# A two-block transformer kernel: order of splits, key scaling and copies in the delta rule, and one wait before out1

## The chip, the cores and the metric

One NeuronCore of a Trainium2 chip runs the whole program, all in fp32. The metric is device microseconds of one execution. The median of three runs of the kernel before is 2344.24 us (2344.18 to 2345.7). Engines: PE is TensorE, DVE VectorE, ACT ScalarE, POOL GpSimd, SP SyncE.

## The reference, cut to what matters

Input x has 512 tokens of 1024 features. A first block has two layers (Fourier and neighbourhood attention, then a gated convolution; each followed by cross attention over 256 memory rows and a convolutional feed-forward). A second block has retention, a gated delta rule and a feed-forward. The two parts that the change touches:

```python
def short_gated_conv_mixer(h, w_in, conv_w, w_out):      # layer 1: in1, then out1
    z = h @ w_in
    gate_b, gate_c, u = z[..., :D], z[..., D:2*D], z[..., 2*D:]
    return (gate_b * dwconv3_centred(gate_c * u, conv_w)) @ w_out

# second block, delta rule: 8 heads of 128, chunks of 128 tokens
qkv = silu(causal_dwconv(concat([dq, dk_, dv_]), dn_conv_w))   # 4 taps per channel
cq, ck = l2norm(cq), l2norm(ck)
g = -exp(dn_a_log) * softplus(da + dn_dt_bias); beta = sigmoid(db)
G = cumsum(g) in a chunk; L = where(causal, exp(G_i - G_j), 0)
A = where(strict, (beta k_i . k_j) * L, 0); attn = (q_i . k_j) * L
T = inverse(I + A)                                  # lower triangular, 128 x 128
u, w = T @ (beta v), T @ (beta k exp(G))
for each chunk: v_new = u - w S; o = q_dec S + attn v_new; S = S d + k_dec^T v_new
```

## The kernel before, in words

**Weights.** Every product with a weight matrix is three fp32r products: w_hi x_hi, w_hi x_lo, w_lo x_hi. Weights come in units of 256 x 512 (512 KB) through a ring of 5 slots (`RING`). For each unit SyncE waits until TensorE has used the slot's last unit and issues the load, ScalarE copies it to `w_hi` (`split`, L624), GpSimd subtracts it for `w_lo` (`lo`, L555), and TensorE does 24 matmuls of 128x512 (`products`, L1067, one line for all: L1081). The units have one order, and each engine does its share in it. ScalarE has the splits between its other work by hand: `split_to(n)` (L630) splits all units before n, and `LEAD` is 4, so `split_to(u + LEAD)` splits up to four units ahead of what TensorE has finished when it has finished u units.

**Engines and semaphores.** Each engine has one queue in program order. All order between engines is by `wait_ge` on counting semaphores; an engine that waits holds all that stands behind it. SyncE's queue holds the weight loads and the DMAs of `diagonal_blocks` and `inverses` (L461, L469), which are placed behind the load of a given unit (L519 to L523).

**The delta stage.** First unit `dab` (projections for beta and decay) and `decay_rows`: ScalarE and VectorE compute rows of 8 x 512, ScalarE stores two of them to `rows_dram`, TensorE transposes four (`decay_columns`, behind the third unit of the first group), ScalarE copies them to TC. `spread(i)` loads the rows of two heads, repeated on all 128 partitions, to GB (1 MB). Then `delta(0)` and `delta(1)`, called half 0 and half 1 here, four heads each. A half has 16 units from `u0 = first["dkqv{q}"]`: keys (u0 to u0+3) into four PSUM banks A, queries (u0+4 to +7) into banks B, then values (+8 to +11) and the `gated` projection (+12 to +15) into B. For keys, queries, values in turn VectorE scales the banks by the norm R into GX (`evacuate`, L2043) and does 16 convolution taps of 128x512 (`taps`, L2049: four multiplies at L2056, twelve multiply-adds at L2059). For keys and queries ScalarE then has silu (L933) and square (L937), TensorE sums the squares into banks A (`squares`, L1427), ScalarE has logarithm and exponential (`inverse_norm`, L939) and VectorE multiplies (`normalise`, L2080). `ages`, `decays` and `with_beta` make the decays DL and AT of two heads at a time. TensorE has `keys_by_keys` (L1438) behind the third unit of the values, `keys_transposed` behind the first unit of `gated` and `keys_by_queries` (L1457) behind its third. VectorE multiplies `keys_by_keys` into AT (L2140); SyncE writes AT to DRAM and reads the 16x16 diagonal blocks back to FSA; VectorE inverts them (`block_inverses`, L2086); SyncE brings them as PKM and PKT (`inverses`), GpSimd spreads them to MM and MT (`expand`, L602), and TensorE and VectorE go by levels to the inverse of 128. ScalarE copies the transposed keys with a factor to KD (`scaled_rows`, L947, line L951), which frees the banks for `keys_by_queries`. At last the scan over four chunks.

**Before out1.** The last two groups of `in1` write banks 0 to 3 and 4 to 7. VectorE scales banks 4 to 7 into TY (L1918), multiplies (L1920), ScalarE copies to YH (L822), VectorE subtracts to YL (L1922). TensorE waits for TY's scaling (L1358) and then starts `out1`, first half into banks 0 to 3, second into 4 to 7.

Of the kernel before, what the change touches and what calls it, by code (L numbers as in the profile page):

```python
# [24 lines left out]
P = 128  # L25
D = 1024
KT = D // P
T = 512
# [65 lines left out]
def program(nc, ins, out):  # L94
    ctx = ExitStack()
    with ctx:
# [67 lines left out]
        def pcol(name, i=0, n=1):  # L164
            c = PARAM_COLS[name][0] + i
            return par[:, c:c + n]
# [281 lines left out]
        def _(sp):  # L448
# [34 lines left out]
            for name, mat, nk, groups in phases:  # L483
# [25 lines left out]
                for g in range(len(groups)):  # L509
# [4 lines left out]
                    for k in range(per):  # L514
# [4 lines left out]
                        for q in range(2):  # L519
                            if u == first[f"gated{q}"] + 3:  # L520
                                diagonal_blocks(q)
                            elif u == first[f"gated{q}"] + 4:
                                inverses(q)  # L523
# [27 lines left out]
        def _(pool):  # L551
# [50 lines left out]
            def expand(q):  # L602
                for i, (pk, m) in enumerate(((PKM, MM), (PKT, MT))):
                    pool.wait_ge(pk_loaded, 16 * (2 * q + i + 1))
                    for hh in range(4):
                        nc.gpsimd.tensor_tensor(
                            m[:, hh, :].rearrange("p (n b c) -> p n b c", n=NCH, c=FIRST),
                            pk[:, 4 * hh:4 * hh + 4, :].unsqueeze(2).broadcast_to([P, NCH, P // FIRST, FIRST]),
                            BD[:, :, :].unsqueeze(1).broadcast_to([P, NCH, P // FIRST, FIRST]), ALU.mult).then_inc(mx_pool, 1)
# [11 lines left out]
        def _(act):  # L621
# [266 lines left out]

            def decay_rows():
# [10 lines left out]
                nc.scalar.activation(sm[0:DN_H, 80:81], pcol("a_log")[0:DN_H, :], ACT.Exp).then_inc(ab_act, 1)  # L900
                act.wait_ge(ab_dve, 9)
# [4 lines left out]
                nc.scalar.dma_start(rows_dram[1], BR[:, :]).then_inc(rows_saved, 16)  # L906
                act.wait_ge(ab_t, 1)
                nc.scalar.activation(TC[:, :, :, :], ps[:, 1, 0:4 * NCH * DN_H].rearrange("p (a n h) -> p a n h", a=4, n=NCH),
                                     ACT.Copy).then_inc(ab_act, 1)

            def spread(i):

                act.wait_ge(rows_saved, 32)
                src = bass.AP(rows_dram.tensor, 2 * i * T, [[0, P], [DN_H * T, 2], [T, 2], [1, T]])
                nc.scalar.dma_start(GB[:, :, :, :], src).then_inc(gb_loaded, 16)

            def delta(q):
# [37 lines left out]
                if q == 0:  # L955
                    decays(0)
                else:
                    split_to(u0 + 2 + LEAD)
                    decays(0)
                    split_to(u0 + 3 + LEAD)  # L960
                    out_norm(0)
# [3 lines left out]
                spread(2 * q + 1)  # L965
                silu(0, KN)
                if q:
                    act.wait_ge(do_n, q)
                square(0, KN, SQk)
                decays(1)  # L970
# [8 lines left out]
                split_to(u0 + 14 + LEAD)  # L979
# [37 lines left out]
            def block2():  # L1017
# [21 lines left out]
                spread(0)  # L1039
# [26 lines left out]
        def _(pe):  # L1066
# [174 lines left out]
            def residual(name, units, xh, xl, ready, after=None):  # L1241
                u = first[name]
                group(u, units, 0, xh, xl, ready, after=after)
                if after is not None:
                    pe.wait_ge(m_ln, 1)
# [96 lines left out]
            for l in range(2):  # L1342
                if l == 0:
                    pe.wait_ge(na_pt, 2 * NA_H)
                    residual("out0", 4, YH, YL, lambda kt: [(f2_lo, kt + 1) if kt < NA_H else (na_lo, kt - NA_H + 1)],
                             after=mem_stat)
                else:
# [10 lines left out]
                    pe.wait_ge(cm_dve, 18 + 16)  # L1358
                    residual("out1", 4, YH, YL, lambda kt: [(cm_dve, 18 * (kt // 4) + 18)])
# [282 lines left out]
        def _(dve):  # L1642
# [391 lines left out]
            def delta(q):  # L2034
# [8 lines left out]
                def evacuate(i):  # L2043
# [3 lines left out]
                    nc.vector.tensor_tensor(GX, banks(inputs[i][2]), over(R[:, :], 4), ALU.mult).then_inc(dq_dve, 1)  # L2047

                def taps(i, start, stop):  # L2049
                    g, dst, _ = inputs[i]  # L2050
                    for n in range(start, stop):
                        back, c = n // 4, n % 4
                        tap = pcol("dn_conv", (3 - back) * 3 * DN_H + g * DN_H + 4 * q + c)
                        if back == 0:
                            dve.wait_ge(dq_dve, nd + 17 * i + 1)
                            nc.vector.tensor_tensor(dst[:, c, :], GX[:, c, :], tap.broadcast_to([P, T]), ALU.mult).then_inc(dq_dve, 1)  # L2056
                        else:
                            dve.wait_ge(dq_dve, nd + 17 * i + n - 2)
                            nc.vector.scalar_tensor_tensor(out=dst[:, c, back:T], in0=GX[:, c, 0:T - back], scalar=tap,  # L2059
# [74 lines left out]
                taps(1, 0, 12)  # L2134
                normalise(0, KN, LNk, 1.0)
                taps(1, 12, 16)
# [293 lines left out]
```

## Time and profile before

| what | value |
|---|---|
| runs | 2344.24 us median (2344.18, 2344.24, 2345.7) |
| profiled execution | 2348.35 us, its span 2346.5 us |
| mean granted TensorE clock | 0.988 of full speed |
| PE, PEld busy | 2280.2 us (97%), 1877.5 us (80%) |
| DVE, ACT, POOL busy | 965.2 (41%), 859.8 (37%), 990.0 (42%) |
| DMA | 222.96 MB, mean 95 GB/s |
| delta stage | about 1487 to 1885 us from the span's start |

The span is from the first to the last recorded instruction of the profiled execution; its own time is 1.85 us longer. An engine is busy while one of its instructions runs. What an engine waited for is put down to the instruction whose semaphore came last. The chain of waits is followed back from the last instruction. Times of rows are microseconds from the span's start.

### The profile page before, as it was taken

Reading aid. Unit: us, or ns where it says so; the run is one execution under the profiler, and the core shown is the slowest. Engines: PE = TensorE matmul, PEld = TensorE weight load, DVE = VectorE, ACT = ScalarE, POOL = GpSimd, SP = SyncE. Lnnn points to the kernel's source line nnn. Section 1 sums busy time; section 2 is a strip of 40 time slices with the busy share of each in tenths; the row PEclk is TensorE's granted clock in tenths of the full one; section 3 lists DMA queues with packets and bytes.
Section 4 is the critical chain, followed back from the end, with each engine's and each line's share of the span. In section 5 each row is a group of like instructions: output and inputs, shape, how many; then the busy total and the mean of one; then the engine's idle time right before and its main releaser. Section 6 shows DMA issues by size and latency. Waiting matters only on the chain.

```text
span 2346.5 us, 24834 instructions
## 1 busy us (share of the span) xinstructions
PE 2280.2 (97%) x10550; PEld 1877.5 (80%) x10550; DVE 965.2 (41%) x1165; ACT 859.8 (37%) x1042; POOL 990.0 (42%) x416
## 2 busy tenths in 40 slices
PE   9999999999999999999999999888998999999997
PEld 7888788888887887888887858777877888888886
DVE  4241324441144213434226441387487332766601
ACT  4354333332322434433345273343352434322221
POOL 5437234544444642444444404244133243464542
PEclk9999999999999999999999999999999999999999
DMA  6325123323332431333333303432131133333332
GB/s 225 95 64 170 54 81 99 98 92 98 99 96 91 154 100 49 95 99 98 92 111 121 95 16 93 112 89 67 56 108 46 53 102 124 99 96 94 98 99 72
DMA packets 159997, 222.96 MB, mean 95 GB/s; under 512 B 24064, under 2 KB 85632, under 8 KB 159632
## 3 DMA queue, kind: packets, MB, share of 16 engines
q1 hardware_dynamic: 158336, 216.63, 30.1%
q10 hardware_dynamic: 1552, 4.76, 0.6%
q8 instruction: 83, 1.36, 0.2%
q14 instruction: 26, 0.21, 0.0%
HBM read 214.50 MB, written 6.85 MB: 94 GB/s over the span
## 4 chain that ended last, share of the span: by engine, by line
PE 89%; DVE 6%; DMA 2%; ACT 2%; issue 1%; POOL 0%; SPq 0%; ACTq 0%; DVEq 0%
PE ps L1081 75%; PE ps L1275 2%; PE ps L1278 2%; PE ps L1291 1%; PE ps L1314 1%; DVE QN L2056 1%; DVE QN L2059 1%; PE ps L1385 1%; PE ps L1463 1%; PE ps L1398 1%; PE ps L1457 1%; PE ps L1438 0%; PE ps L1589 0%; DMA w_raw<-w_in 0%; DVE FSU L2096 0%
## 5 line engine op out<-in xcount | busy, mean ns | idle before, releaser
L559 POOL TENSOR_TENSOR w_lo<-w_raw,w_hi 128x1024 fp32r<-128x1024 f32 x378 | 959.1, 2547 | 1313.4 <-ACT w_hi L628 1313.1
L628 ACT ACTIVATE w_hi<-w_raw 128x1024 fp32r<-128x1024 f32 x378 | 394.9, 1056 | 896.0 <-DMA w_raw<-w_in 140.7
L1081 PE MATMUL ps<-XH,w_hi 128*128 128x512 f32 x1784 | 701.7, 393 | 15.2 <-POOL w_lo L559 13.2
L1081 PE MATMUL ps<-XH,w_lo 128*128 128x512 f32 x1784 | 696.2, 390 | 0.0
L1081 PE MATMUL ps<-XL,w_hi 128*128 128x512 f32 x1784 | 695.8, 390 | 0.0
L1081 PE MATMUL ps<-HID,w_hi 128*128 128x512 f32 x1728 | 534.5, 391 | 2.5 <-DVE TY L1918 2.4
L1081 PEld LDWEIGHTS ps<-XH,w_hi 128*128 128x128 f32 x1784 | 336.0, 188 | 89.7 <-issue 17.6
L1081 PEld LDWEIGHTS ps<-XL,w_hi 128*128 128x128 f32 x1784 | 336.0, 188 | 71.3 <-issue 2.4
L1081 PEld LDWEIGHTS ps<-XH,w_lo 128*128 128x128 f32 x1784 | 335.7, 188 | 70.1
L1081 PEld LDWEIGHTS ps<-HID,w_hi 128*128 128x128 f32 x1728 | 325.0, 188 | 71.3 <-DVE TY L1918 2.8
L1081 PE MATMUL ps<-HID,w_lo 128*128 128x512 f32 x864 | 336.9, 390 | 0.0
L1679 DVE TENSOR_TENSOR H<-ps,H 128x512 f32<-128x512 f32 x64 | 42.4, 683 | 362.7 <-PE ps L1081 311.7
L1081 PEld LDWEIGHTS ps<-HID,w_lo 128*128 128x128 f32 x864 | 162.5, 188 | 34.0
L1855 DVE TENSOR_TENSOR GP<-ps,R 128x1024 f32<-128x1024 f32 x16 | 19.6, 1224 | 179.0 <-PE ps L1081 179.0
L1806 DVE TENSOR_TENSOR QX<-ps,R 128x2048 f32<-128x2048 f32 x4 | 9.2, 2291 | 157.3 <-PE ps L1081 157.3
L2235 DVE SCALAR_TENSOR_TENSOR CV<-GP,par,CV 128x512 f32<-128x512 f32 x88 | 72.0, 888 | 0.0
L2227 DVE TENSOR_TENSOR GP<-ps,R 128x2048 f32<-128x2048 f32 x11 | 25.2, 2292 | 76.6 <-PE ps L1081 76.6
L638 ACT ACTIVATE SQ<-H 128x512 f32<-128x512 f32 x56 | 35.3, 631 | 55.3 <-DVE ACC L1651 30.3
L810 ACT ACTIVATE EG<-CV,par 128x512 f32<-128x512 f32 x32 | 22.2, 725 | 85.7 <-DVE CV L1864 85.7
L1651 DVE TENSOR_TENSOR ACC<-ACC,SQ 128x512 f32<-128x512 f32 x62 | 45.0, 726 | 3.2 <-ACT SQ L638 0.9
L1864 DVE SCALAR_TENSOR_TENSOR CV<-GP,par,CV 128x512 f32<-128x512 f32 x64 | 43.7, 740 | 0.0
L1873 DVE TENSOR_TENSOR HID<-HF,HID 128x1024 fp32r<-128x1024 f32 x16 | 35.5, 2219 | 18.0 <-ACT HID L814 18.0
(356 smaller groups left out, 2259.8 us busy)
## 6 DMA issues: line engine op xcount, KB each, us to landing
w_raw<-w_in SPq DMA_DIRECT2D x72, 512.0 KB, 3.8
w_raw<-ffn_w_up SPq DMA_DIRECT2D x128, 256.0 KB, 2.9
w_raw<-w_up SPq DMA_DIRECT2D x88, 256.0 KB, 3.1
w_raw<-xa_wkv SPq DMA_DIRECT2D x32, 512.0 KB, 3.7
w_raw<-ffn_w_down SPq DMA_DIRECT2D x32, 512.0 KB, 3.8
w_raw<-w_in_c SPq DMA_DIRECT2D x24, 512.0 KB, 3.8
w_raw<-w_down SPq DMA_DIRECT2D x22, 512.0 KB, 3.8
w_raw<-xa_wq SPq DMA_DIRECT2D x16, 512.0 KB, 3.8
```

The source lines that it names most:

```text
L559: nc.gpsimd.tensor_tensor(w_lo[:, s, :, :], w_raw[:, s, :, :], w_hi[:, s, :, :].bitcast(F32), ALU.subtract).then_inc(lo_done, 1)
L628: nc.scalar.activation(w_hi[:, s, :, :], w_raw[:, s, :, :], ACT.Copy).then_inc(hi_done, 1)
L638: nc.scalar.activation(ACC[:, :] if c == 0 else SQ[:, :], H[:, c, :], ACT.Square).then_inc(sq_done, 1)
L1081: mm = nc.tensor.matmul(ps[:, bank + m, :], a, b, start=start and j == 0 and n == 0, stop=stop and j == 1 and n == 2)
L1275: mm = nc.tensor.matmul(ps[:, bank + m, 0:NMEM], wt[:, m * P:(m + 1) * P], xt, start=begin, stop=end)
L1278: mm = nc.tensor.matmul(ps[:, bank + m, :], xt[:, m * P:(m + 1) * P], wt, start=begin, stop=end)
L1651: nc.vector.tensor_tensor(ACC[:, :], ACC[:, :], SQ[:, :], ALU.add).then_inc(acc_done, 1)
L1679: nc.vector.tensor_tensor(H[:, c, :], ps[:, (c + flip) % 8, :], H[:, c, :], ALU.add).then_inc(h_upd, 1)
L1864: nc.vector.scalar_tensor_tensor(out=CV[:, q, :], in0=GP[:, q, i:T + i], scalar=tap(i, q), in1=CV[:, q, :], op0=ALU.mult, op1=ALU.add).the ...
L1873: nc.vector.tensor_tensor(HID[:, 2 * g + nf:2 * g + nf + 2, :], HF[:, :, :], HID[:, 2 * g:2 * g + 2, :].bitcast(F32), ALU.subtract).then_i ...
L2227: nc.vector.tensor_tensor(GP4[:, :, 2:T + 2], banks(bank), over(R[:, :], 4), ALU.mult).then_inc(up2_dve, 1)
L2235: nc.vector.scalar_tensor_tensor(out=CV4[:, q, :], in0=GP4[:, q, i:T + i], scalar=of(w0 + 2 * nf * i, q), in1=CV4[:, q, :], op0=ALU.mult, ...
```

## The change

ScalarE gets splits at new places: two between the decay rows, and single ones ahead of `decays(0)` of half 0, of the keys' silu and of `decays(1)`; one split fewer stands ahead of the KD copies. `spread(0)` moves ahead of the `TC` copy. The keys are scaled in place in PSUM (`banks(A)`) and tapped from there; queries and values go by GX as before. `normalise` of the keys follows 6 taps of the queries and not 12. On SyncE `inverses` moves behind the load of the next unit, and GpSimd waits for PKM and PKT together. `out1` waits for TY's scaling ahead of its second half; ahead of its first it waits for the bank's own reader.

```diff
--- before.py
+++ after.py
@@ -519,7 +519,7 @@
                         for q in range(2):
                             if u == first[f"gated{q}"] + 3:
                                 diagonal_blocks(q)
-                            elif u == first[f"gated{q}"] + 4:
+                            elif u == first[f"gated{q}"] + 5:
                                 inverses(q)
                         if name == "out0" and (g, k) == (0, per - 1):
 
@@ -601,7 +601,7 @@
             pool.wait_ge(vc_done, 8)
             def expand(q):
                 for i, (pk, m) in enumerate(((PKM, MM), (PKT, MT))):
-                    pool.wait_ge(pk_loaded, 16 * (2 * q + i + 1))
+                    pool.wait_ge(pk_loaded, 32 * (q + 1))
                     for hh in range(4):
                         nc.gpsimd.tensor_tensor(
                             m[:, hh, :].rearrange("p (n b c) -> p n b c", n=NCH, c=FIRST),
@@ -886,6 +886,12 @@
                         act.wait_ge(ret_ro, h)
                     nc.scalar.activation(RN[:, :], RLN[:, :], ACT.Exp, scale=-0.5).then_inc(ret_rn, 1)
 
+            def spread(i):
+
+                act.wait_ge(rows_saved, 32)
+                src = bass.AP(rows_dram.tensor, 2 * i * T, [[0, P], [DN_H * T, 2], [T, 2], [1, T]])
+                nc.scalar.dma_start(GB[:, :, :, :], src).then_inc(gb_loaded, 16)
+
             def decay_rows():
 
                 B1, A1, A3, SPR, BEG, EGL, EG8 = [rows[i][:, :] for i in (0, 1, 2, 3, 4, 5, 6)]
@@ -898,21 +904,18 @@
                 act.wait_ge(ab_act, 3)
                 nc.scalar.activation(A3, A3, ACT.Ln, bias=1.0).then_inc(ab_act, 1)
                 nc.scalar.activation(sm[0:DN_H, 80:81], pcol("a_log")[0:DN_H, :], ACT.Exp).then_inc(ab_act, 1)
+                split_to(first["dab"] + 2 + LEAD)
                 act.wait_ge(ab_dve, 9)
                 nc.scalar.activation(EG8, GR[:, :], ACT.Exp).then_inc(ab_act, 1)
                 act.wait_ge(ab_dve, 14)
                 nc.scalar.activation(EGL, EGL, ACT.Exp).then_inc(ab_act, 1)
                 nc.scalar.dma_start(rows_dram[0], GR[:, :]).then_inc(rows_saved, 16)
                 nc.scalar.dma_start(rows_dram[1], BR[:, :]).then_inc(rows_saved, 16)
+                spread(0)
+                split_to(first["dab"] + 3 + LEAD)
                 act.wait_ge(ab_t, 1)
                 nc.scalar.activation(TC[:, :, :, :], ps[:, 1, 0:4 * NCH * DN_H].rearrange("p (a n h) -> p a n h", a=4, n=NCH),
                                      ACT.Copy).then_inc(ab_act, 1)
-
-            def spread(i):
-
-                act.wait_ge(rows_saved, 32)
-                src = bass.AP(rows_dram.tensor, 2 * i * T, [[0, P], [DN_H * T, 2], [T, 2], [1, T]])
-                nc.scalar.dma_start(GB[:, :, :, :], src).then_inc(gb_loaded, 16)
 
             def delta(q):
                 u0 = first[f"dkqv{q}"]
@@ -953,6 +956,7 @@
                         last.then_inc(rows_act, 1)
 
                 if q == 0:
+                    split_to(u0 + 3 + LEAD)
                     decays(0)
                 else:
                     split_to(u0 + 2 + LEAD)
@@ -963,10 +967,12 @@
                 act.wait_ge(dp_eg, 4 * q + 2)
                 act.wait_ge(dp_be, 4 * q + 2)
                 spread(2 * q + 1)
+                split_to(u0 + 6 + LEAD)
                 silu(0, KN)
                 if q:
                     act.wait_ge(do_n, q)
                 square(0, KN, SQk)
+                split_to(u0 + 7 + LEAD)
                 decays(1)
                 split_to(u0 + 8 + LEAD)
                 inverse_norm(0, LNk)
@@ -976,7 +982,7 @@
                 square(1, QN, SQq)
                 split_to(u0 + 12 + LEAD)
                 inverse_norm(1, LNq)
-                split_to(u0 + 14 + LEAD)
+                split_to(u0 + 13 + LEAD)
                 act.wait_ge(dp_be, 4 * q + 4)
                 act.wait_ge(dp_eg, 4 * q + 4)
                 scaled_rows(KD, 3, 16 * q + 4)
@@ -1036,7 +1042,6 @@
                                          ACT.Sigmoid).then_inc(gr_act, 1)
                 split_to(first["dab"] + 1 + LEAD)
                 decay_rows()
-                spread(0)
                 delta(0)
                 delta(1)
                 for g in range(2):
@@ -1238,11 +1243,11 @@
                     fourier(s + 2)
             values(2 * NA_H - 1)
 
-            def residual(name, units, xh, xl, ready, after=None):
+            def residual(name, units, xh, xl, ready, after=None, second=None):
                 u = first[name]
                 group(u, units, 0, xh, xl, ready, after=after)
-                if after is not None:
-                    pe.wait_ge(m_ln, 1)
+                if second is not None:
+                    pe.wait_ge(*second)
                 group(u + units, units, 4, xh, xl)
 
             def mem_stat():
@@ -1343,7 +1348,7 @@
                 if l == 0:
                     pe.wait_ge(na_pt, 2 * NA_H)
                     residual("out0", 4, YH, YL, lambda kt: [(f2_lo, kt + 1) if kt < NA_H else (na_lo, kt - NA_H + 1)],
-                             after=mem_stat)
+                             after=mem_stat, second=(m_ln, 1))
                 else:
                     u0 = first["in1"]
                     for g in range(6):
@@ -1355,8 +1360,9 @@
 
                                 pe.wait_ge(cm_dve, 18 * ((g - 2) // 3) + (1, 2, 16)[(g - 2) % 3])
                             group(u0 + 4 * g, 4, 4 * (g % 2), XH, XL)
-                    pe.wait_ge(cm_dve, 18 + 16)
-                    residual("out1", 4, YH, YL, lambda kt: [(cm_dve, 18 * (kt // 4) + 18)])
+                    pe.wait_ge(cm_dve, 18 + 2)
+                    residual("out1", 4, YH, YL, lambda kt: [(cm_dve, 18 * (kt // 4) + 18)],
+                             second=(cm_dve, 18 + 16))
                 kv(l)
 
                 pe.wait_ge(kv_out, 4 * l + 3)
@@ -2044,19 +2050,21 @@
                     dve.wait_ge(w_used, u0 + 4 * i + 4)
                     if nd + i:
                         dve.wait_ge(dq_dve, nd + 17 * i)
-                    nc.vector.tensor_tensor(GX, banks(inputs[i][2]), over(R[:, :], 4), ALU.mult).then_inc(dq_dve, 1)
+                    x = banks(A) if i == 0 else GX
+                    nc.vector.tensor_tensor(x, banks(inputs[i][2]), over(R[:, :], 4), ALU.mult).then_inc(dq_dve, 1)
 
                 def taps(i, start, stop):
                     g, dst, _ = inputs[i]
+                    x = banks(A) if i == 0 else GX
                     for n in range(start, stop):
                         back, c = n // 4, n % 4
                         tap = pcol("dn_conv", (3 - back) * 3 * DN_H + g * DN_H + 4 * q + c)
                         if back == 0:
                             dve.wait_ge(dq_dve, nd + 17 * i + 1)
-                            nc.vector.tensor_tensor(dst[:, c, :], GX[:, c, :], tap.broadcast_to([P, T]), ALU.mult).then_inc(dq_dve, 1)
+                            nc.vector.tensor_tensor(dst[:, c, :], x[:, c, :], tap.broadcast_to([P, T]), ALU.mult).then_inc(dq_dve, 1)
                         else:
                             dve.wait_ge(dq_dve, nd + 17 * i + n - 2)
-                            nc.vector.scalar_tensor_tensor(out=dst[:, c, back:T], in0=GX[:, c, 0:T - back], scalar=tap,
+                            nc.vector.scalar_tensor_tensor(out=dst[:, c, back:T], in0=x[:, c, 0:T - back], scalar=tap,
                                                            in1=dst[:, c, back:T], op0=ALU.mult, op1=ALU.add).then_inc(dq_dve, 1)
 
                 def ages(pr):
@@ -2131,9 +2139,9 @@
                 ages(1)
                 evacuate(1)
                 with_beta(1)
-                taps(1, 0, 12)
+                taps(1, 0, 6)
                 normalise(0, KN, LNk, 1.0)
-                taps(1, 12, 16)
+                taps(1, 6, 16)
                 for hh in range(4):
                     dve.wait_ge(kv_pe, 16 * q + hh + 1)
                     dve.wait_ge(dp_be, 4 * q + hh + 1)
```

## Rows read from the trace of the kernel before

**Rows 1.** The page, part 1: busy us (share of the span) and instructions.

```profile
PE 2280.2 (97%) x10550; PEld 1877.5 (80%) x10550; DVE 965.2 (41%) x1165; ACT 859.8 (37%) x1042; POOL 990.0 (42%) x416
```

**Rows 2.** TensorE's waits, whole span: us in total, times, longest.

```profile
PE ps L1081 <- DVE TY L1918: 2.4, 1, 2.4
```

**Rows 3.** The same waits, stretch 1480 to 1670 (half 0).

```profile
PE ps L1081 <- POOL w_lo L559: 10.1, 2, 8.3
PE ps L1457 <- ACT KD L951: 5.8, 1, 5.8
PE ps L1438 <- DVE KN L2083: 4.9, 1, 4.9
```

**Rows 4.** The same waits, stretch 1670 to 1860 (half 1).

```profile
PE ps L1457 <- ACT KD L951: 7.3, 1, 7.3
PE ps L1081 <- POOL w_lo L559: 3.1, 1, 3.1
PE ps L1438 <- DVE KN L2083: 1.9, 1, 1.9
```

**Rows 5.** A stretch: length, busy PE, PEld, DVE, ACT, POOL, PEclk, DMA share, GB/s.

```profile
1775.00:1789.00 14.00, 7.07 (x36) 6.97 (x37) 6.24 (x10) 10.26 (x21) 11.26 (x8) 0.63 0.25 92
```

**Rows 6.** The chain of waits in the delta stage: start, us, what.

```profile
1492.35 16.32 PE ps L1081 x72
...
1509.80 6.93 DMA GB<-rows_dram
...
1523.68 24.04 PE ps L1081 x96
...
1574.50 6.01 PE ps L1438 x32
...
1581.25 5.04 DMA at_dram<-AT
...
1602.53 5.44 DMA w_raw<-w_in
...
1613.32 5.39 PE ps L1457 x32
...
1626.58 3.84 PE ps L1463 x32
...
1742.14 5.45 PE ps L1438 x32
...
1781.93 6.37 PE ps L1457 x32
```

**Rows 7.** ScalarE in order of time: start, us, line, tiles [idle before].

```profile
1500.41 0.20 ACT L900 ACTIVATE sm<-par 8x1 f32<-8x1 f32 x1
...
1520.06 3.88 ACT L628 ACTIVATE w_hi<-w_raw 128x1024 fp32r<-128x1024 f32 x4
...
1608.96 4.22 ACT L951 ACTIVATE KD<-ps,TC 128x128 f32<-128x128 f32 x16
```

**Rows 8.** GpSimd in order of time.

```profile
1550.02 16.88 POOL L559 TENSOR_TENSOR w_lo<-w_raw,w_hi 128x1024 fp32r<-128x1024 f32 x6 [18.12 <-ACT w_hi L628]
...
1618.48 5.06 POOL L606 TENSOR_TENSOR MT<-PKT,BD 128x512 f32<-128x512 f32 x4
```

**Rows 9.** VectorE in order of time.

```profile
1553.33 11.32 DVE L2056 TENSOR_TENSOR QN<-H,par 128x512 f32<-128x512 f32 x4
...
1603.80 2.35 DVE L2083 SCALAR_TENSOR_TENSOR QN<-QN,LNq 128x1024 f32<-128x1024 f32 x2
...
1702.63 8.00 DVE L2059 SCALAR_TENSOR_TENSOR KN<-H,par,KN 128x511 f32<-128x511 f32 x12
```

**Rows 10.** Two VectorE lines reading PSUM: ns min/median/max, first and last start.

```profile
L1679 DVE TENSOR_TENSOR H<-ps,H x64: 673/682/692, 157.4 to 2332.5; 128x512 f32<-128x512 f32 x64
...
L1985 DVE SCALAR_TENSOR_TENSOR RO<-ps,par,RN x8: 739/742/751, 1362.8 to 1401.5; 128x512 f32<-128x512 f32 x8
```

**Rows 11.** VectorE in order of time, before out1.

```profile
740.57 2.29 DVE L1922 TENSOR_TENSOR HID<-TY,HID 128x2048 fp32r<-128x2048 f32 x1 [1.98 <-ACT HID L822]
```

## The prediction

> **What bounds the kernel now.** Read first the busy row of the page: TensorE is busy 97% of the span [rows 1], so a change can save only what TensorE idles, or what it runs slowly. Next the waits of TensorE, over the span and then in each half of the delta stage: one wait of 2.4 us before `out1` [rows 2]; in half 0, 10.1 us for `w_lo` in two waits (8.3 the longest, so 1.8 the other), 5.8 us for KD and 4.9 us for the normalised keys [rows 3]; in half 1, 3.1, 7.3 and 1.9 us [rows 4]. Together 35.5 us. The third view is the table of stretches: around the 7.3 us wait the mean granted clock is 0.63 [rows 5], that is, most of the stretch lies at 1.2 GHz and not at 2.4, behind an idle TensorE. So a wait costs more than its length. The chain of waits prices that [rows 6]. 72 matmuls take 16.32 us, 0.227 each; the 96 after the first wait take 24.04, where 96 x 0.227 = 21.8 would do: 2.2 over, with no wait among them (the 1.8 us wait comes behind them, at unit `u0`+8). `keys_by_keys` takes 6.01 us behind its wait (5.45 in half 1), `keys_by_queries` 5.39 and 6.37, while 32 matmuls of the same shape with no wait ahead take 3.84: 2.2, 1.6, 1.55 and 2.5 over. In half 1 72 matmuls behind the `w_lo` wait run some 1.8 over by the same slow clock (an estimate, from the 2.2). Slow clock in all 11.9 us. **The ceiling is 35.5 + 11.9 = 47.4 us.**
>
> **Splits between decay rows.** ScalarE, which makes `w_hi`, makes none between unit `dkqv0`+3 and 1520.06, then four in a row [rows 7], since it stands in `decay_rows`, `spread` and `decays` waiting for others. TensorE has used up its four units at 1515.3 and waits 8.3 us. The changed order splits unit `u0`+4 behind the `a_log` exponential (which starts at 1500.41 [rows 7]); the slot was freed when `dab` was used at 1492.35 [rows 6], eight microseconds before, and even the load issued at 1602.53 had landed 5.44 us later, so the data are there. One split is 0.97 us (3.88 for four [rows 7]) and GpSimd's `w_lo` 2.8 at most (16.88 for six [rows 8]), so the unit is ready at about 1504.4. The three that follow are ready by 1508, 1511 and 1520.6, and TensorE needs them from 1515.3, each 5.45 later. The wait and its slow clock go: 10.5 us. The 1.8 us wait of unit `u0`+8 goes too: it is now split before the keys' silu and not in the burst behind `decays(1)`. Cost on ScalarE: the 0.97 us falls before its wait for VectorE's scan, so nothing, and 0.97 at most on the decay rows. `spread(0)` no longer stands behind the `TC` copy; it was issued at 1509.80 [rows 6], and the rows stored at 1504.6 should have landed by some 1506.6 (bounds 1505 and 1509). GB takes 6.9 us to land, so 1513.5 in place of 1516.7. What it moves past is the `TC` copy alone, at 1509.8, which still waits for the transposes; TensorE's wait for it has 5 us of slack.
>
> **Keys scaled and tapped in PSUM.** The scaled keys stay in the bank. No row shows VectorE writing to PSUM. Bounds against the scaling as it is: 0.7 us less (nothing lands in SBUF) and 2.3 more (twice the time); I take 0, since the scaling of the same shape into SBUF, which the chain of half 1 holds, is the nearest. Tapping from PSUM: a multiply with PSUM input takes 0.68 us, a fused multiply-add 0.74 [rows 10]; the SBUF taps of half 1 take 8.00 for twelve, 0.67 apart [rows 9]. Equal. What it buys is independence from GpSimd. The four first query taps take 11.32 us beside the burst of `w_lo` [rows 8, 9], 2.83 each, one per GpSimd instruction, and 2.2 above 0.67. The PSUM row is never above 0.692 in 64 instances, some of them beside a `w_lo` [rows 10]. So the keys' 16 taps take 10.5-11 us although GpSimd now works among them.
>
> On this the Trainium skill ("SBUF — State Buffer", Who interferes with whom) says a VectorE instruction with two SBUF inputs and a GpSimd instruction that reads SBUF block each other for a whole instruction, one with a single SBUF input does not; by it the taps in PSUM cannot be held up, and the trace agrees (0.692 against 2.83). A rule against the change is in "VectorE: DVE Perf Modes" (The TRN2 errata): a PSUM source costs 120 cycles and an SBUF source 58, at 0.96 GHz. By that 16 taps would cost 1.0 us more per half, and the sum would be about 1 us worse; the rows (0.68, 0.74 at either source) show none of it, and I go by the rows.
>
> Does the keys' chain hold? Half 0: GB 1513.5, two ages 2.8, scaling 2.2, AT 1.2 plus one collision 2.2, 16 taps 10.7: 1532.6; silu and square 3.9: 1536.5. TensorE, without its waits, asks at 1515.3 + 21.8 = 1537.1. Half 1: the chain is unchanged (TensorE did not wait there) and 0.9 us early. Both are near: if the PSUM taps cost 0.1 us more each, 0.7 to 1.2 us are lost per half.
>
> **Keys normalised sooner.** Normalising now follows 6 query taps and not 12; it waited behind two or more GpSimd collisions. New time in half 0: scaling 1539.4, AT with beta 1542.6 (after `decays(1)`, 1541.4), six taps 3.9 and one collision 2.2, so 1548.7; the logarithm and exponential on ScalarE end 1549; the keys are ready at 1551-1553. TensorE arrives after squares 3.5 and 72 matmuls at 1556.9. Both waits and the slow clock go: 4.9 + 2.2 and 1.9 + 1.6 us. What is late next: ten more taps, 6.7 and one or two collisions, end near 1561.5, where `keys_by_keys` ends 1560.8; AT at 1564.2, query squares ready 1565.3, TensorE asks at 1566.2.
>
> **Transposed keys copied ahead of a split.** The KD copies start at 1608.96 because ScalarE stood before the split of unit `u0`+17, whose load SyncE issued only at 1602.53 [rows 6, 7], after `inverses`. Now the load goes first and KD needs no such split; the copies (4.22 us) start about 1577.9, behind the transposes. TensorE asks at 1587.9: 5.8 + 1.55 and 7.3 + 2.5 us are uncovered. SyncE's price: unit `u0`+18's load waits for the inverses, and TensorE needs it some 40 us later: nothing. Waiting for both PKM and PKT delays `expand` by the 0.4 us between two issues; `level_inner` is 10 us later: nothing.
>
> **What takes its place.** From the last AT (DMA to `at_dram` starts 1581.25 [rows 6]) to the end of the queries' normalising (1603.80 + 2.35 [rows 9]) are 24.9 us: two DMAs, the block inverses, eight taps. TensorE has 27.0 us from the end of `keys_by_keys`. Once its waits are gone VectorE is last: AT now ends 3.4 us behind `keys_by_keys` in half 0 and about 4 in half 1, so 24.9 + 3.4 - 27.0 = 1.3 and 2.0 us, and one more `w_lo` (unit `u0`+17) falls into the chain, up to 2.2. I take 2.5 and 3.2. Behind it `expand`, eight GpSimd instructions of 1.27 us (5.06 for four [rows 8]), now lies beside the values' taps and no longer beside ATT from PSUM: 0 to 5 us on VectorE, of which 2 are covered; I take 2 for each half. The waits that are left (2 us or so) keep a little slow clock, 0.5 each time: bounds 0 (all at full clock) and 2.5. Given back in all: half 0 2.5 + 2 + 0.5 = 5, half 1 3.2 + 2 + 0.5 = 5.7.
>
> **out1.** Its first half writes banks 0 to 3, freed long before; the wait for TY (2.4) goes. TensorE then asks for the second four tiles of YL 10.9 us after `in1`'s end; VectorE has them 733.9 to 742.9, 9.0 later [rows 11]. So 2.4, with 1.9 us of cover left. The layer-0 call is the same as before.
>
> **Sum.** 47.4 - 10.7 = 36.7 us. The profiled execution took 2348.35 (span 2346.5 and 1.85 around it), which gives 2311.6; it stands 4.1 above the median of the runs, 2344.24, and against this, the time asked for, the forecast is **2307.5 us**.
>
> **Rivals.** (a) VectorE keeps up everywhere: 2344.2 - 47.4 = 2297. For it: a collision has two sides, and where it falls on GpSimd, which has slack, VectorE loses nothing. Against: 24.9 + 3.4 is more than 27.0. 18%. (b) VectorE becomes the bound outright: each of some six `w_lo` and eight `expand` instructions per half stops a tap; 13 us per half given back, not 5.3, gain 21: 2323. For it: 2.83 per tap [rows 9]. Against: `w_lo` now comes one per 5.45 us and not in bursts. 18%. (c) Slower: VectorE in PSUM is held up by TensorE's writes to the neighbouring banks, each tap at the 2.83 seen in a collision: 32 x 2.2 = 70 us, 2344.2 - 36.7 + 69 = 2376. It decides from 36.7 / 32 = 1.15 us more per tap. Against: 64 PSUM reads at 0.692 or less while TensorE ran. 2%. (d) It doesn't do what it says: a split moved forward meets a load not landed and delays the decay rows, so the first 10.5 stay and others with them: gain 0 to 12, about 2336. Against: the slots were free 8 us earlier. 4%. The forecast keeps 58%, its own range 2301 to 2315.
>
> **Range and chances.** 2296 to 2327 takes in (a) and most of (b). A measurement here tells about 0.2% (4.7 us) from nothing. Faster 0.96, within 0.02 (half of (d)), slower 0.02.
>
> **What would show it.** Right: no `w_lo` wait near 1515; KD copies start within 2 us of the transposes; taps from PSUM at 0.67 spacing with `w_lo` beside them; the chain passes VectorE's inverses and the queries' normalising into `keys_by_queries`, with 1 to 4 us of wait; PEclk above 0.9 in the whole stage. Wrong: a wait of `squares(0)` for SQk over 2 us, taps above 0.8 us, or a wait on `cm_dve` inside `out1`.

## The result, and the profile after

The changed kernel takes **2319.14 us** (median of four runs, 2317.8 to 2319.82), the kernel before 2344.64 beside it (2344.18 to 2345.7): ratio 0.9887, 95% interval 0.9875 to 0.99 (the two medians alone give 0.9891). It is faster by 25.5 us. The forecast was 2307.5, a gain of 36.7. The result lies in the whole range, 2296 to 2327, but 4.1 us outside the forecast's own, 2301 to 2315, and next to rival (b), 2323. The profiled execution took 2317.8 (span 2316.0), 30.5 us less than the profiled one of before, which stood 3.7 above the median of 2344.64 where this one stands 1.3 below its own.

The busy row of the page, to be held against [rows 1]: TensorE does the same 10550 instructions in 10 us less.

```profile
PE 2270.0 (98%) x10550; PEld 1870.5 (81%) x10550; DVE 966.2 (42%) x1165; ACT 860.3 (37%) x1042; POOL 993.3 (43%) x416
```

TensorE's waits in the whole span (us in total, times, longest), against [rows 2 to 4]. Every wait of the delta stage in those groups is gone (the `w_lo` wait left here stands at 1276, before it). Two new kinds have come: for ATT, the products of queries and keys times the decays, ahead of the values' transposes (L1451), and for the normalised queries QN (L1463).

```profile
PE ps L1451 <- DVE ATT L2156: 11.5, 2, 6.5
PE ps L1463 <- DVE QN L2091: 5.3, 2, 2.8
...
PE ps L1086 <- POOL w_lo L559: 2.5, 1, 2.5
```

The stretches around them (length, busy PE, PEld, DVE, ACT, POOL, granted clock, DMA share, GB/s), against [rows 5]. The first holds the waits of half 0, the second those of half 1. The third is a piece of half 1 as long as that of [rows 5] (14 us): a clock of 0.76 where 0.63 stood. The forecast's sign "PEclk above 0.9 in the whole stage" failed.

```profile
1581.00:1608.00 27.00, 17.72 (x117) 15.98 (x116) 24.00 (x21) 9.43 (x20) 20.47 (x10) 0.87 0.19 57
...
1745.00:1766.00 21.00, 15.87 (x79) 14.58 (x80) 18.19 (x14) 8.83 (x20) 18.19 (x10) 0.78 0.13 41
...
1755.00:1769.00 14.00, 9.05 (x51) 8.52 (x50) 9.96 (x11) 7.09 (x18) 8.19 (x4) 0.76 0.13 37
```

The chain of waits of half 0 (start, us, what), against [rows 6]. Up to the values' transposes it now runs mostly over VectorE, and its longest piece there is eight taps of the values, 13.44 us.

```profile
1502.01 5.84 DMA GB<-rows_dram
...
1518.56 7.89 DVE KN L2067 x12
...
1557.11 5.04 DMA at_dram<-AT
...
1581.93 2.27 DVE QN L2091 x2
1584.20 13.44 DVE VB L2067 x8
1598.17 1.88 DVE ATT L2156 x3
1600.10 3.47 PE ps L1451 x16
```

VectorE and GpSimd in order of time (start, us, line, tiles, count, [idle before]), against [rows 8, 9]. The keys, scaled in PSUM (2.30 us) and tapped there, take 0.66 us a tap although two `w_lo` of GpSimd start at 1517.82. The values, tapped from SBUF beside `expand`, take 1.69 a tap, and `expand` takes 15.4 us for its eight, where they are 5.06 for four when alone [rows 8].

```profile
1510.97 2.30 DVE L2054 TENSOR_TENSOR ps<-ps,R 128x2048 f32<-128x2048 f32 x1
...
1518.48 7.95 DVE L2067 SCALAR_TENSOR_TENSOR KN<-ps,par,KN 128x511 f32<-128x511 f32 x12
...
1584.13 13.52 DVE L2067 SCALAR_TENSOR_TENSOR VB<-H,par,VB 128x510 f32<-128x510 f32 x8
```

```profile
1517.82 4.78 POOL L559 TENSOR_TENSOR w_lo<-w_raw,w_hi 128x1024 fp32r<-128x1024 f32 x2 [2.80 <-ACT w_hi L628]
...
1574.79 2.75 POOL L559 TENSOR_TENSOR w_lo<-w_raw,w_hi 128x1024 fp32r<-128x1024 f32 x1 [2.67 <-ACT w_hi L628]
1581.76 8.62 POOL L606 TENSOR_TENSOR MM<-PKM,BD 128x512 f32<-128x512 f32 x4 [4.23 <-DMA PKT<-m_dram]
1590.34 6.75 POOL L606 TENSOR_TENSOR MT<-PKT,BD 128x512 f32<-128x512 f32 x4
```

On this the Trainium skill ("SBUF — State Buffer", Who interferes with whom) says that a VectorE instruction with two SBUF inputs and a GpSimd instruction that reads SBUF hold each other up, and one with a single SBUF input is free of it. The trace agrees on both: 1.69 us a tap with two SBUF inputs, 0.66 with one input in PSUM (beside `w_lo`).

ScalarE's KD copies start 0.9 us behind the start of the keys' transposes, 39 us sooner than in [rows 7] (some 6 of them were won ahead of the stage):

```profile
1569.55 4.21 ACT L954 ACTIVATE KD<-ps,TC 128x128 f32<-128x128 f32 x16
```

### The profile page after: what moved, and what is told of

It reads as the page before. It is cut to its first block, busy times and chain, and to the rows that moved or that the text cites. A ratio compares the mean times of both kernels' runs of the same rounds, so it can differ in the third digit from the quotient of the medians.

```text
span 2316.0 us, 24835 instructions
## 1 busy us (share of the span) xinstructions
PE 2270.0 (98%) x10550; PEld 1870.5 (81%) x10550; DVE 966.2 (42%) x1165; ACT 860.3 (37%) x1042; POOL 993.3 (43%) x416
## 3 DMA queue, kind: packets, MB, share of 16 engines
q8 instruction: 83, 1.36, 0.2%
## 4 chain that ended last, share of the span: by engine, by line
PE 86%; DVE 9%; ACT 3%; DMA 1%; issue 1%; POOL 0%; ACTq 0%; DVEq 0%
PE ps L1086 72%; PE ps L1280 2%; PE ps L1283 2%; DVE VB L2067 1%; PE ps L1296 1%; PE ps L1319 1%; DVE QN L2067 1%; PE ps L1469 1%; PE ps L1391 1%; PE ps L1404 1%; DVE KN L2067 1%; PE ps L1595 0%; DMA at_dram<-AT 0%; DVE MT L2175 0%; DVE QN L2064 0%
```

## The experiments

The ratio is to the kernel before in the same session, whose medians were 2346.09 (a), 2346.14 (b) and 2345.27 (c1, d). The changed kernel's own session had 2344.64, so a difference between sessions is good to some 1.5 us only.

**a1. out1 alone.** The kernel before with only this (shortened; `residual` takes the new argument as in the change):

```diff
-                    pe.wait_ge(cm_dve, 18 + 16)
+                    pe.wait_ge(cm_dve, 18 + 2)
-                    residual("out1", ...)
+                    residual("out1", ..., second=(cm_dve, 18 + 16))
```

> The kernel before with the out1 edit alone. Theory: TensorE's 2.35 us wait for TY goes, and with it the 1.75 us by which the 192 matmuls behind it ran over at the lower clock (45.27 us against 43.5), so 2.4 to 4.1 us under before's 2344.6: 2340.5 to 2342.3. Rival: the wait comes back inside out1, at the fifth tile of YL (VectorE has it 9.0 us after in1's end, TensorE asks at 10.9): within 0.5 us of before, and a wait on VectorE's HID shows in TensorE's waits.

Measured 2343.83 us (2342.6 to 2345.63), ratio 0.999 (0.9981 to 0.9999). It is 2.3 us under before in its session, where 2.4 to 4.1 were expected. The interval takes in 0.2 to 4.5 us, so the run agrees with the forecast's 2.4 and can't tell it from 4.1. The rival is out: between 715 and 810 us TensorE waits for nothing.

**a2. Keys by SBUF.** The changed kernel, but the keys are scaled to GX and tapped from it:

```diff
-                    x = banks(A) if i == 0 else GX
+                    x = GX
```

> The changed kernel with the keys scaled into SBUF (GX) and tapped from there, all else as changed. Theory: two w_lo instructions now fall among the keys' taps in each half and each stretches one tap by 2.2 us; TensorE, which had 0.8 us to spare at the squares of the keys, waits about 3.6 us per half there: 2323 to 2327. Rival (PSUM is as good as SBUF and protects nothing that counts): 2318 to 2320, and no wait of L1436 for SQk. Rival (the PSUM taps themselves cost more per tap): under 2318.

Measured 2328.02 us (2326.55 to 2328.95), ratio 0.9919 (0.9906 to 0.9931), 1 us above the range of the theory: the place in PSUM is worth 8.9 us by the medians, 7.5 by the ratios. VectorE's rows of half 0 in this kernel, then its four multiplies of half 0 in the kernel before, and TensorE's waits in a2:

```profile
1517.64 4.70 DVE L2063 TENSOR_TENSOR KN<-H,par 128x512 f32<-128x512 f32 x4
1522.27 10.15 DVE L2066 SCALAR_TENSOR_TENSOR KN<-H,par,KN 128x511 f32<-128x511 f32 x12
```

```profile
1526.78 6.88 DVE L2056 TENSOR_TENSOR KN<-H,par 128x512 f32<-128x512 f32 x4
```

```profile
PE ps L1451 <- DVE ATT L2155: 6.6, 1, 6.6
PE ps L1436 <- ACT SQk L940: 3.9, 1, 3.9
```

Two collisions with the low halves make the sixteen taps 4.4 us longer than the 10.4 of the changed kernel, and a wait for the keys' squares comes up, 3.9 us here and 3.6 in half 1. In half 1 this is the change's own doing: its splits put GpSimd beside keys' taps that ran free before (8.00 for twelve, [rows 9]). In half 0 the keys' taps of the kernel before met the burst of `w_lo` as well (6.88 us for the four multiplies, 2.47 in the changed kernel), so there the PSUM place removes a collision that was old.

**a3. Expansion behind the values' taps.** One wait more on GpSimd:

```diff
             def expand(q):
+                pool.wait_ge(dq_dve, 51 * (q + 1))
```

> The changed kernel with one more wait on GpSimd: expand starts when VectorE has done the values' last tap. Theory (the 6.5 and 4.9 us that TensorE waits for ATT before the values' transposes come from expand and the values' taps blocking each other: the last eight taps take 13.5 us where 5.35 would do): the eight taps take 5.35 us, the two waits fall under 1 us, and with the lower clock behind them 9 to 13 us go: 2306 to 2310. Rival (the late MM and MT turn into a new wait at the level products): the waits move to L1469 or L1478 and the time stays within 2317 to 2321.

Measured **2305.15 us** (2303.82 to 2310.27), ratio 0.9826 (0.9809 to 0.9842): 14 us faster than the changed kernel, 0.9 more than expected. VectorE and GpSimd in half 0, and all that TensorE waits for there:

```profile
1584.34 5.36 DVE L2068 SCALAR_TENSOR_TENSOR VB<-H,par,VB 128x510 f32<-128x510 f32 x8
```

```profile
1589.83 5.09 POOL L607 TENSOR_TENSOR MM<-PKM,BD 128x512 f32<-128x512 f32 x4 [12.69 <-DVE VB L2068]
1594.87 4.95 POOL L607 TENSOR_TENSOR MT<-PKT,BD 128x512 f32<-128x512 f32 x4
```

```profile
PE ps L1464 <- DVE QN L2092: 3.0, 1, 3.0
PE ps L1470 <- DVE H L1948: 0.6, 1, 0.6
```

The eight taps are back at 0.67 each, both ATT waits (6.5 and 4.9 us) are gone, and `expand` beside ATT from PSUM takes no longer than alone. The 14.0 us are these 11.4 and, as the rest, most likely the slow clock behind them. This shows the cause of the missing gain: one order wait gives back more than the 11.2 us that were missing.

**a4. Keys normalised later again**, behind twelve query taps:

```diff
-                taps(1, 0, 6)
+                taps(1, 0, 12)
```

> The changed kernel with the keys normalised behind twelve query taps, as before the change. Theory (with the w_lo instructions spread out, VectorE is late by its whole list of work and not by the keys' place in it): the keys come at about 1552.2 instead of 1543.8, TensorE waits some 1.2 us at keys_by_keys, but AT still ends within 0.5 us of where it does: 2319 to 2321. Rival (sooner normalising is worth what the waits for KN cost before, 7.1 and 3.5 us): 2326 to 2330.

Measured 2318.31 us (2317.73 to 2319.95), ratio 0.9879 (0.9865 to 0.9893): no difference. The wait for KN doesn't come back, not even the 1.2 us of the theory: the keys are ready at 1548.0 and `keys_by_keys` starts at 1551.0.

**b1. No early splits.** The changed kernel, with the splits between the decay rows and the one ahead of `decays(0)` of half 0 taken out and `spread(0)` back in its place (only the lines taken out are shown). The splits ahead of the keys' silu and of `decays(1)` stay, in both halves:

```diff
-                split_to(first["dab"] + 2 + LEAD)
-                spread(0)
-                split_to(first["dab"] + 3 + LEAD)
-                    split_to(u0 + 3 + LEAD)
```

> The changed kernel with one part undone: the splits of the weights that stand between the decay rows (and the early one of half 0) go back behind them. In the kernel before, TensorE waited 8.3 and 1.9 us there for the low halves of the weights, and the part was priced at 10.5 us in half 0 and 1.8 us in half 1 (waits with the slow clock behind them). Theory, nothing else takes the time up: some 11 us above the changed kernel's 2319, 2328 to 2333. Rival, the waits further down (6.5 and 4.9 us for ATT on VectorE) shrink by the same, since VectorE's chain starts from the decay rows, which come some 2 us sooner without the splits: 2319 to 2325.

Measured 2327.42 us (2324.89 to 2327.79), ratio 0.9918 (0.9905 to 0.9932), 8.3 above the changed kernel (7.3 by the ratios), between the two ranges. The expectation misreads one price: the 1.8 us belong to the wait for unit `u0`+8 of half 0, and this run doesn't undo the split that removed it. TensorE's waits in half 0:

```profile
PE ps L1083 <- POOL w_lo L559: 7.6, 1, 7.6
PE ps L1448 <- DVE ATT L2153: 6.5, 1, 6.5
PE ps L1460 <- DVE QN L2088: 0.8, 1, 0.8
```

The wait of [rows 3] is back, 7.6 for 8.3. Of the rival only 2 us is true: QN's wait shrinks from 2.8 to 0.8, ATT's doesn't (in half 1 it grows, 6.6 for 4.9).

**b2. Transposed keys behind the split.** The changed kernel with

```diff
-                            elif u == first[f"gated{q}"] + 5:
+                            elif u == first[f"gated{q}"] + 4:
                                 inverses(q)
-                split_to(u0 + 13 + LEAD)
+                split_to(u0 + 14 + LEAD)
```

> The changed kernel with the copies of the transposed keys put behind the split again (and the inverses one unit sooner, as before). In the kernel before, TensorE waited 5.8 and 7.3 us for KD; the part was priced with the slow clock at 7.35 and 9.8 us. Theory: the wait comes back ahead of the keys' products, from which VectorE's chain to ATT starts as well, so that nothing downstream makes it good: 14 to 18 us above the changed kernel, 2333 to 2337. Rival: TensorE arrives later at the values' transposes, where it waits 6.5 and 4.9 us for ATT anyway, and these waits shrink: 2322 to 2328.

Measured 2316.82 us (2315.81 to 2318.47), ratio 0.9876 (0.9862 to 0.9889). Both ranges missed: undoing the part costs nothing. TensorE's waits in half 0, then GpSimd:

```profile
PE ps L1463 <- ACT KD L954: 7.3, 1, 7.3
PE ps L1469 <- DVE H L1947: 0.6, 1, 0.6
```

```profile
1587.21 5.14 POOL L559 TENSOR_TENSOR w_lo<-w_raw,w_hi 128x1024 fp32r<-128x1024 f32 x1 [12.50 <-ACT w_hi L628]
1592.32 4.94 POOL L606 TENSOR_TENSOR MM<-PKM,BD 128x512 f32<-128x512 f32 x4
```

The KD wait is back (7.3 and 7.2 us), and the waits for ATT and QN, 16.8 in all, are gone. Here the load of the unit behind `inverses` lands late, ScalarE's split and GpSimd's `w_lo` with it, and `expand`, which stands behind that `w_lo` in GpSimd's queue, starts at 1592, when the values' taps are over (they take 5.37 us here; it is the `w_lo` beside them that takes 5.14 for 2.4). The order of before had kept `expand` off the taps by the very lateness that the change removes.

**b4. Expansion as in a3, queries normalised first:**

```diff
-                taps(2, 0, 8)
                 normalise(1, QN, LNq, float(P) ** -0.5)
-                taps(2, 8, 16)
+                taps(2, 0, 16)
```

> GpSimd's expansion behind the values' taps, as in a3 (2305), and in addition the queries normalised ahead of all the values' taps. In a3 TensorE waits 3.0 and 2.5 us for QN and for nothing else of the two halves over 1 us; VectorE does 4.7 + 2.7 us of values' taps before QN. Theory: both waits go, with about 1 us of slow clock: 2298 to 2302, and ATT is as soon as before, the order alone being changed. Rival: QN's factor from ScalarE is not there sooner, or the matmuls behind then run into ATT: 2303 to 2307.

Measured **2300.41 us** (2298.97 to 2301.12), ratio 0.9805 (0.9791 to 0.9818), as expected: the fastest version run, 18.7 us under the changed kernel and 4.7 under a3. In half 0 TensorE waits for two things, and the granted clock is 1.00 in the stretch that had 0.87:

```profile
PE ps L1452 <- DVE ATT L2156: 1.5, 1, 1.5
PE ps L1470 <- DVE H L1948: 0.2, 1, 0.2
```

```profile
1581.00:1608.00 27.00, 25.16 (x187) 23.09 (x186) 24.81 (x37) 9.45 (x20) 14.54 (x10) 1.00 0.26 64
```

**b5. Expansion as in a3, transposed keys behind the split as in b2.**

> GpSimd's expansion behind the values' taps, as in a3 (2305), with the copies of the transposed keys behind the split again. Here no wait for ATT is left that could hide the wait for KD. If the forecast's price of 17.2 us for this part holds: 2320 to 2324. If the price was too high because the wait of the kernel before partly stood for work that VectorE had to do anyway (the wait for QN, 5.5 us in all, goes with it): 2313 to 2318. The difference between b2 and b5 is then what the ATT wait hides.

Measured 2315.5 us (2314.49 to 2316.64), ratio 0.987 (0.9856 to 0.9883). With `expand` off the taps the early KD copies are worth 10.4 us (2315.5 - 2305.15), in the second range: KD's waits are 7.0 and 7.4 us, and QN's 5.5 are hidden behind them. The difference to b2 is 1.3 us, within the noise, since in b2 `expand` was out of the way already.

**c1. Queries normalised first, `expand` left beside the taps** (b4's diff on the changed kernel).

> The changed kernel with the queries normalised ahead of all the values' taps, and GpSimd's expansion where the changed kernel has it. Theory: VectorE's string up to ATT is what TensorE waits for in both halves; QN's waits (2.8 and 2.5 us) go and the waits for ATT grow by as much: 2317 to 2320. Rival: QN's wait is time of its own that is won whatever GpSimd does: 2312 to 2315.

Measured 2322.8 us (2322.17 to 2323.34), ratio 0.9904 (0.9888 to 0.9921): 3.7 slower than the changed kernel, worse than either theory. QN's waits are gone, ATT's are 11.7 and 11.4 us for 6.5 and 4.9: nearly all of the values' twelve multiply-adds now lie beside GpSimd, and the queries' normalising beside a `w_lo` (4.56 us for 2.35).

```profile
1575.78 4.56 DVE L2091 SCALAR_TENSOR_TENSOR QN<-QN,LNq 128x1024 f32<-128x1024 f32 x2
1580.27 2.49 DVE L2064 TENSOR_TENSOR VB<-H,par 128x512 f32<-128x512 f32 x4
1582.67 18.26 DVE L2067 SCALAR_TENSOR_TENSOR VB<-H,par,VB 128x511 f32<-128x511 f32 x12
```

**d1. Before, with the splits and out1 only; d2, the same with the keys in PSUM.** Built from the changed kernel by the edits of a2, a4 and b2 (d1), and of a4 and b2 (d2). So both keep all five new splits, the earlier `spread(0)` and GpSimd's joint wait for PKM and PKT.

> The kernel before with two parts of the change, the earlier splits and out1's waits by tile; the keys still go by GX in SBUF and are normalised after twelve query taps, the transposed keys are copied behind the split. Forecast by the prediction's price for the splits (12.3 us) and a1's 2.3: 2331. Theory from b1 (8.3 us with everything else in place) and a2 (keys by SBUF, whose taps ran beside the low halves: 10.15 us for 7.95): the low halves now fall on the keys' taps, part of the gain is lost there: 2333 to 2339. Rival: the splits' gain is as forecast or more, 2329 to 2332.

> d1 with the keys scaled in PSUM and tapped there; the changed kernel less its two other moves (keys normalised sooner, transposed keys copied ahead of the split). Theory: each of these two, undone alone, cost nothing (a4 2318.3, b2 2316.8, the changed kernel 2319.1), and they do not stand in for each other, since the wait for KN is gone by the taps in PSUM: 2315 to 2320. Rival: one hides what the other leaves, and undone together they cost what the forecast gave the keys normalised sooner, up to 10.6 us: 2325 to 2330.

d1: 2325.86 us (2324.58 to 2328.81), ratio 0.9919 (0.9904 to 0.9934), below both ranges. Less a1's 2.3, the splits (with `spread(0)` and the joint wait) give 17.1 us of the 19.4. The four first query taps, 11.32 us beside the burst in [rows 9], take 4.68, the waits for KN are gone (4.0 and 3.6 us for SQk stand in their place), and KD's stays. d2: 2315.44 us (2314.38 to 2319.32), ratio 0.9876 (0.9861 to 0.9891), as expected: 10.4 us less than d1. Keys normalised sooner and KD copied sooner add nothing to it: the changed kernel is 3.7 us above by the medians, 2.6 by the ratios, whose intervals overlap. TensorE's waits of half 0 in d1, then in d2:

```profile
PE ps L1463 <- ACT KD L954: 5.2, 1, 5.2
PE ps L1436 <- ACT SQk L940: 4.0, 1, 4.0
```

```profile
PE ps L1463 <- ACT KD L954: 7.8, 1, 7.8
PE ps L1469 <- DVE H L1947: 0.6, 1, 0.6
```

**b3. Before, once more**, one execution.

> The kernel before, unchanged, for a second profile. In the first one the granted clock was 0.91 in 725 to 745 and in 1270 to 1290 us, and the time 4 us above the median. If a wait of 2.4 us always brings the slow clock, both stretches show 0.91 again and the time is 2348; if it does so in some executions only, one or both show 1.00 and the time is 2344 to 2346.

2346.12 us. The two stretches, first in this profile, then in the first one of before:

```profile
725.00:745.00 20.00, 17.62 (x72) 14.07 (x71) 9.45 (x7) 4.99 (x4) 8.33 (x4) 0.91 0.22 71
1270.00:1290.00 20.00, 17.52 (x78) 14.20 (x77) 11.90 (x8) 12.71 (x12) 12.07 (x5) 1.00 0.27 81
```

```profile
725.00:745.00 20.00, 17.62 (x72) 14.13 (x71) 9.99 (x7) 4.98 (x4) 8.76 (x4) 0.91 0.24 73
1270.00:1290.00 20.00, 17.55 (x70) 14.03 (x70) 11.48 (x8) 13.12 (x11) 11.68 (x5) 0.91 0.26 68
```

The same wait of 2.4 us at 1278 brought the slow clock in one and not in the other, and the 288 matmuls behind it took 67.19 and 65.56 us. Of the fourteen profiles of this case four show 0.91 there, ten 1.00. In the first stretch, with the wait for TY of 2.4 us, both profiles of before show 0.91, and the two kernels with out1's new wait (a1 and the changed one) 1.00.

## Why the prediction was right in sign and short in size

The gain came, 25.5 us of 36.7. The whole range held only because it was drawn round rival (b) too; the forecast's own range missed by 4.1 us, and the step that failed is the price of `expand` beside the values' taps.

**The ceiling and its waits: right.** All waits of [rows 2 to 4] went, and in a1 the out1 term measured 2.3 for 2.4 (0.2 to 4.5). In the two profiled executions the landmarks (the first matmul behind each wait) put 17.2 us of the gain into half 0, 7.3 into half 1, 4.1 at out1 (the slow clock there, 1.75, had been left out of the sum) and 2.0 ahead of the stage, where the clock differed by chance. Forecast were 21.8, 12.5 and 2.4. The halves are 9.8 us short.

**The new splits: right in sum, in part by luck.** The prediction prices 12.3 us under this head, all in half 0. Its ceiling holds 4.9 more for half 1 (the `w_lo` wait of 3.1 and 1.8 of slow clock), and its sum keeps them without saying what removes them; in the traces it is the splits ahead of silu and of `decays(1)`, which stand in both halves. So the sum has 17.2 us for the splits, and d1 measured 17.1. But these are not the same waits: the spread splits also free the query taps and with them the normalised keys, which the prediction paid under another head, and the keys' taps in SBUF take some back (SQk, 7.6 us). b1 takes only the three splits of half 0 out, priced at 10.5: 8.3 measured. Its waits were as read, 7.6 for 8.3. What ScalarE does sooner fell into place: the changed times lie 6 us ahead for what was won before the stage, and with that GB was forecast for 1507.4 (1507.87) and the end of the keys' taps for 1526.5 (1526.4). One small cost was not forecast: the early `w_lo` lies beside the scan, four instructions in 3.51 us instead of 1.36.

**Keys in PSUM: right.** Cost 0 (2.30 us for 2.29, taps 0.66), and it protects the taps: 8.9 us in a2, 10.4 between d1 and d2. The sum had no term of its own for this.

**Keys normalised sooner: the waits went, for another reason.** 10.6 us forecast, 0 measured (a4): with the splits spread, the later place is early enough. In d2 the keys are normalised at 1550.5, and `keys_by_keys` starts at 1553.5; in d1, with the keys in SBUF, there is no wait for KN either, though TensorE comes 4 us later there for SQk. The term belonged to the parts above, and there it shows.

**What takes its place: this step failed, by the size of `expand` beside the values' taps.** The prediction took 0 to 5 us on VectorE, 2 covered, so 2 a half. It is 8.2 us (13.52 for 5.36), and TensorE waits 6.5 and 4.9, with slow clock behind it: 7.4 us of wait more than the 2 a half that were priced. The cover was sized right (8.2 less 6.5 leaves 1.7 in half 0), the overlap was not. Rival (b) let every GpSimd instruction stop a tap and came nearer by it, but its price of 2.2 each, from the longer `w_lo` of [rows 8, 9], is too high for `expand`: eight of them cost 8.2 us, about 1 each. The other term there was right: TensorE waits 2.8 and 2.5 us for the queries, forecast 2.5 and 3.2. The chain from the last AT to the normalised queries took 27.1 us, 24.9 plus one collision.

**Transposed keys ahead of a split.** Forecast 17.2 uncovered; with all 10.7 given back put down to this part, 6.5 net. Measured nothing (b2), as the give-back is 16.8 us of waits. It is worth 10.4 us once `expand` is behind the taps (b5), so its worth rests on the place of one GpSimd step, which the prediction saw moving and priced too low.

**The signs.** Those of being right held but for two: the chain's waits on VectorE were not only for the queries' normalising, where 1 to 4 us were forecast (2.8 and 2.5), but for the values' taps and ATT behind it; and the clock fell under 0.9. None of the signs of being wrong showed: no wait for SQk over 2 us, no PSUM tap above 0.8 us apart, no wait inside `out1`.

Left open: by how much the slow clock adds to each wait (it differs between executions), and the 1 to 4 us by which d2 may beat the changed kernel.

## What to carry to other kernels

Before a late transfer or split is moved ahead, ask what stands behind it on every engine's queue and was held off by its lateness; here GpSimd's expansion came 10 us sooner, fell on VectorE's taps and gave back all that the move had won. Where two engines collide, the time of both one after the other is a price that fits here (5.4 + 10.0 us, measured 15.4 for the two together); give it in full to the engine on the critical path until a run says otherwise. If an order wait can keep them apart, try it: in a3 it brought no new wait over 0.6 us. Gains don't add up: the early KD copies were worth nothing with `expand` beside the taps and 10.4 us without (b2, b5), and queries first cost 3.7 us in the one case (c1) and won 4.7 in the other (b4). So a part is judged on the version in which it will stand.

## What was not expected of the hardware

- VectorE multiplying in place in PSUM takes 2.30 us for 128x2048, from PSUM to SBUF 2.29.
- The scan on 8 partitions, with two SBUF inputs, is held up by GpSimd as well: 3.51 us for four beside one `w_lo` of 2.44, 1.36 without. VectorE in the changed kernel, GpSimd in it, and VectorE in the kernel before:

```profile
1494.90 3.51 DVE L2030 TENSOR_TENSOR_SCAN GR<-row,row 8x128 f32<-8x128 f32 x4
```

```profile
1495.39 2.44 POOL L559 TENSOR_TENSOR w_lo<-w_raw,w_hi 128x1024 fp32r<-128x1024 f32 x1 [7.37 <-ACT w_hi L628]
```

```profile
1501.15 1.36 DVE L2024 TENSOR_TENSOR_SCAN GR<-row,row 8x128 f32<-8x128 f32 x4
```

- A collision can cost both sides or one. Eight taps took 13.5 us for 5.4 and eight expansions beside them 15.4 for 10.0, so both end nearly as if they had run one after the other (5.4 + 10.0). In b2 one `w_lo` beside the same eight taps took 5.14 us for 2.4, and the taps 5.37: there GpSimd alone paid. No run shows what decides it.
- Behind a wait of some 2.4 us at the same place (1278) TensorE's granted clock fell (0.91 over 20 us, so partly at 1.2 GHz) in four profiles and stayed at 2.4 GHz in ten.
